# State-space inputs computed with channels on partitions and reloaded in place, and one block of the memory split a slot sooner, in a four-layer decoder trunk

## The chip, the cores and the metric

The kernel runs on one core of one Trainium2 chip, in one launch. The metric is the device time of the whole program in microseconds (us). Unmarked times are us from the start of the profiled span, or durations.

## What is computed

256 tokens of width 2048 pass through two layers, each with a mixer, a cross-attention into 256 memory tokens and an MLP of width 8192; all is float32. The first mixer is attention and retention. The second, in which most of the change lies, takes 1024 channels `u` of its input projection into a state-space bank (64 groups of 16 channels, 64 complex states each) and the rest into a gated short convolution. Cut to what matters:

```
def odd_mixer(xn, w_in, ...):
    proj = xn @ w_in
    u, h, gb, gc = jnp.split(proj, cuts, axis=-1)
    ssm = s5_mixer(u, a_re, a_im, b_re, b_im, c_re, c_im, d_skip, log_step, w_glu)
    conv = short_conv_mixer(h, gb, gc, conv_w).astype(xn.dtype)
    return jnp.concatenate([ssm, conv], axis=-1) @ w_out

# in s5_mixer: one group's channels c, states p, tokens l
    bu = jnp.einsum('blgc,gpc->blgp', uf.astype(jnp.complex64), b_bar)
    # states: x[l] = a_bar * x[l-1] + bu[l]
    y = jnp.einsum('blgp,gcp->blgc', states, c_mat).real + d_skip.astype(F32) * uf
```

At the start, `memn = rmsnorm(mem, norm_mem)` is projected by `xa_wkv` for the keys and values of both layers' cross-attention.

## The kernel before

**Weights.** Every projection streams its weights in units of 4 MB. A unit is eight halves of 512 KB, in a ring of four halves (`RING`). For each half ACT makes `whi`, the weight rounded to float32r (`split`, L1288), DVE makes `wlo = raw - whi` (L1854), and PE multiplies `x_hi*whi + x_hi*wlo + x_lo*whi`. SP loads raw slabs of two halves (L404) when the halves they replace are split. PE waits for `lo_ready` before each half; ACT may split half n once PE has finished half n-4. All the engines' programs are written out by hand, one slot for each half, and each engine works its own list in order. So what an engine waits for in a slot stands ahead of its part in the next half's weights.

**Kinds of unit.** "full" (L619 to L645) has tokens on the output's partitions: 12 matmuls of 128x512 for a half, into one bank pair of `acc`. "wide" (L1059 to L1088) and "heads" (`hidden_unit`, L1090 to L1112) have the output's channels on partitions, the weights stationary, and `x_hi`, `x_lo` side by side as the 512 moving columns: 8 matmuls of 128x512 and 8 of 128x256 for a half. Their two halves of 256 columns are then added by DVE (`hidden_sum`, L2214 and L2223). A wide unit fills two banks of `at` and one pair of `acc`, a heads unit four banks of `acc`. Both are used in the MLP: each MLP opens with a wide unit and goes on with a heads unit.

**The odd mixer.** Its projection is eight units (`O_UNITS`), the first two for `u`; t counts their halves from 0, eight to a unit. A row's 1/rms (`rstd` row 4) is ready only late in the first unit, so it scales the outputs. Before the change all eight are full. The two `u` units come out with tokens on partitions, ACT scales them into `onat` (L1306), POOL writes them to DRAM (`uc_d`, L2727), SP reads them back 128 rows at a time (`Ucb`, L543), PE turns each by two transposes (`s5_u`, L1176, after halves t = 25 to 32), ACT copies them to `UT` (L1704), and PE multiplies `UT` by the tables (`s5_x`, tile `at`, L726, after halves 27 to 34). SP's loads of the tables `et_d` (L548) wait for PE's earlier `s5_x`.

**The start.** The first unit (`first_unit`) projects the memory. PE turns the memory's four blocks of 512 columns (L702) between halves: block 0 before half 0, block 1 after half 0, block 2 after half 2, block 3 after half 4. ACT and DVE split each turned block (`hi_parts` L1320, `lo_parts` L1874) in a slot of their own; the second, block 1, in slot 2. After half 1 PE also turns the rows of gains (L742, L743) into the same two banks of `tp`, and needs them free.

The few lines that order the split of the memory's blocks on ACT:

```
    if u == 0 and i == 0:
        hi_parts(yt, 0, MEM, (1,))
    if u == 0 and i in (2, 4, 6):
        hi_parts(yt, 2 * i, MEM)
```

Of the kernel before, what the change touches and what calls it, by code (L numbers as in the profile page):

```python
# [105 lines left out]
def trunk(nc, x, mem, norm_mix, norm_xattn, norm_mlp, norm_mem, norm_final, ab_w_in, ab_b_forget,  # L106
# [4 lines left out]
    with ctx:  # L111
# [104 lines left out]
        Ucb = [view(4160 + 256 * b, 256, "p (r w) -> p r w", r=2) for b in range(3)]  # L216
# [34 lines left out]
        uc_d = nc.dram_tensor("uc_d", [G, L, GC], F32, kind="Internal").ap()  # L251
# [50 lines left out]
        uc_in, et_in = ([sem(f"{n}{b}") for b in range(3)] for n in ("uc_in", "et_in"))  # L302
# [35 lines left out]
        at_before_x = at_before_tab + 16  # L338
# [4 lines left out]
        tp_before_u = 3 + 2 * (4 + 4 + 2 + 8 + 2) + 8 + 16 + 2 * 12 + 8  # L343
# [52 lines left out]
        def _(sp):  # L396
# [53 lines left out]
            def factor_loads(s):  # L450
# [82 lines left out]
            def s5_loads(s):  # L533

                ks = [k for k in (s - X8_T - 6, s - X8_T - 5) if 0 <= k < 8]
                for k in ks:
                    if k == 0:
                        sp.wait_ge(u_out, 64)
                        for b in range(2):
                            sp.wait_ge(et_out[b], 16 * 8)  # L540
                    if k >= 3:
                        sp.wait_ge(tp_full, tp_before_u + k - 2)
                    sp.dma_start(Ucb[k % 3], uc_d.rearrange("(s q) (j i) c -> (q j) s (i c)", s=2, i=T8)[  # L543
                        P * k:P * (k + 1)]).then_inc(uc_in[k % 3], 16)
                for k in ks:
# [20 lines left out]
            for o, (name, g) in enumerate(O_UNITS):  # L566
                load("full", cd_w_in[0], [O_COL[name] + g * NB], hook=lambda i, o=o: s5_loads(8 * o + 2 * i))
# [2226 lines left out]
```

## Time and profile before

| what | value |
|---|---|
| median of 3 runs | 2427.01 us (2426.27 to 2429.1) |
| the profiled execution's own time | 2426.3 us |
| its span | 2424.5 us |
| mean granted TensorE clock | 0.998 |
| PE busy | 2407.5 us, 99% of the span |
| DVE, ACT, POOL busy | 1478.8, 1189.2, 362.2 us (61%, 49%, 15%) |
| DMA | 488.96 MB, mean 202 GB/s |

The profiled execution took 2426.3 us, 1.8 us more than its span; the sum of the prediction is made against it. PE is busy nearly all the time, so the time is the sum of what PE does and the little that it waits. Rows of the timeline merge neighbouring instructions of one kind: start, duration from the first's start to the last's end, engine, line, output and inputs, count, and in brackets the idle time before with what ended it. Matmuls overlap, so the pace is the distance between starts.

### The profile page before, as it was taken

How to read it: one execution, taken by the hardware profiler on the slowest of the kernel's cores; microseconds unless marked ns; L12 is line 12 of the kernel's file. 1: busy time of each engine (PE TensorE's matmuls, PEld its weight loads, DVE VectorE, ACT ScalarE, POOL GpSimd, SP SyncE). 2: the span in 40 equal slices, each digit the busy share in tenths (PEclk: the TensorE clock that was granted, in tenths of full speed). 3: DMA queues.
4: the chain of work that ended last, by engine and by line, in shares of the span. 5: the costliest groups of instructions: out<-in, count | busy, mean ns of one | idle time of the engine just before them, and what ended most of it. 6: DMA issues, size and time to landing. Idle time of an engine off the chain costs nothing.

```text
span 2424.5 us, 32116 instructions
## 1 busy us (share of the span) xinstructions
PE 2407.5 (99%) x12596; PEld 2023.5 (83%) x12596; DVE 1478.8 (61%) x1856; ACT 1189.2 (49%) x1583; POOL 362.2 (15%) x480
## 2 busy tenths in 40 slices
PE   9999999999999999999999999999999999999998
PEld 7878888888888888888888887788888888888887
DVE  5546554556665556888866457566755655555555
ACT  6544455546544444444445444556644444444444
POOL 0033120010564002555510100000000000000000
PEclk9999999999999999999999999999999999999999
DMA  8655555574566567787785768955565565565563
GB/s 303 213 175 180 183 205 173 161 204 141 191 191 191 190 200 222 240 260 242 249 270 178 204 230 240 264 191 155 193 191 191 190 190 190 190 190 190 190 191 122
DMA packets 335593, 488.96 MB, mean 202 GB/s; under 512 B 18517, under 2 KB 175093, under 8 KB 335349
## 3 DMA queue, kind: packets, MB, share of 16 engines
q1 hardware_dynamic: 316804, 461.47, 59.5%
q0 software_dynamic: 3920, 12.84, 2.0%
q10 hardware_dynamic: 14752, 13.05, 1.6%
q8 instruction: 79, 1.29, 0.2%
q14 instruction: 38, 0.30, 0.0%
HBM read 471.39 MB, written 20.13 MB: 203 GB/s over the span
## 4 chain that ended last, share of the span: by engine, by line
PE 93%; DVE 3%; ACT 2%; DMA 1%; issue 1%; SPq 0%; ACTq 0%; DVEq 0%
PE acc L635 19%; PE acc L637 19%; PE acc L636 19%; PE acc L1104 18%; PE acc L1107 9%; PE tp L702 2%; PE at L726 2%; DVE wlo L1854 1%; ACT whi L1288 1%; PE acc L1076 1%; PE at L1076 1%; ACT arena L1452 1%; PE tp L726 0%; DMA raw<-in_xa_wkv 0%; DMA arena<-uc_d 0%
## 5 line engine op out<-in xcount | busy, mean ns | idle before, releaser
L1854 DVE TENSOR_TENSOR wlo<-raw,whi 128x1024 fp32r<-128x1024 f32 x824 | 1043.5, 1270 | 834.7 <-ACT whi L1288 831.1
L1288 ACT ACTIVATE whi<-raw 128x1024 fp32r<-128x1024 f32 x824 | 871.2, 1061 | 978.0 <-PE acc L637 597.2
L635 PE MATMUL acc<-whi,yt_hi 128*128 128x512 f32 x1408 | 553.3, 393 | 0.7 <-DVE h L1891 0.4
L637 PE MATMUL acc<-whi,yt_lo 128*128 128x512 f32 x1408 | 548.4, 389 | 0.0
L636 PE MATMUL acc<-wlo,yt_hi 128*128 128x512 f32 x1408 | 548.2, 389 | 0.0
L1104 PE MATMUL acc<-x,whi 128*128 128x512 f32 x1920 | 481.7, 393 | 0.0
L1104 PEld LDWEIGHTS acc<-x,whi 128*128 128x128 f32 x1920 | 345.9, 189 | 64.3 <-issue 1.6
L635 PEld LDWEIGHTS acc<-whi,yt_hi 128*128 128x128 f32 x1408 | 264.4, 188 | 57.3 <-issue 2.0
L637 PEld LDWEIGHTS acc<-whi,yt_lo 128*128 128x128 f32 x1408 | 264.3, 188 | 55.7
L636 PEld LDWEIGHTS acc<-wlo,yt_hi 128*128 128x128 f32 x1408 | 264.5, 188 | 53.1
L635 PE MATMUL acc<-whi,x 128*128 128x512 f32 x736 | 292.8, 398 | 0.9 <-DVE wlo L1854 0.9
L637 PE MATMUL acc<-whi,x 128*128 128x512 f32 x736 | 287.1, 390 | 0.0
L636 PE MATMUL acc<-wlo,x 128*128 128x512 f32 x736 | 286.6, 389 | 0.0
L1107 PEld LDWEIGHTS acc<-x,wlo 128*128 128x128 f32 x1920 | 261.9, 190 | 18.7
L1107 PE MATMUL acc<-x,wlo 128*128 128x256 f32 x1920 | 267.7, 282 | 0.0
L2480 POOL TENSOR_TENSOR arena<-arena 128x32 f32<-128x32 f32 (+5 forms) x275 | 191.0, 695 | 319.5 <-DMA arena<-fp_d 181.2
L635 PEld LDWEIGHTS acc<-whi,x 128*128 128x128 f32 x736 | 138.2, 188 | 32.4 <-DVE wlo L1854 4.0
L637 PEld LDWEIGHTS acc<-whi,x 128*128 128x128 f32 x736 | 138.1, 188 | 29.6
L636 PEld LDWEIGHTS acc<-wlo,x 128*128 128x128 f32 x736 | 138.4, 188 | 27.2
L2750 POOL TENSOR_TENSOR arena<-h,arena 128x1024 f32<-128x1024 f32 x2 | 5.7, 2846 | 662.1 <-DVE h L1891 662.1
L1891 DVE SCALAR_TENSOR_TENSOR h<-acc,rstd,h 128x512 f32<-128x512 f32 x124 | 87.0, 743 | 0.0
L2223 DVE TENSOR_REDUCE arena<-acc 128x256 f32<-128x512 f32 x124 | 84.7, 683 | 0.0
(240 smaller groups left out, 1517.8 us busy)
## 6 DMA issues: line engine op xcount, KB each, us to landing
raw<-in_mlp_w SPq DMA_DIRECT2D x256, 1024.0 KB, 5.6
raw<-in_ab_w_in SPq DMA_DIRECT2D x56, 1024.0 KB, 4.9
raw<-in_cd_w_in SPq DMA_DIRECT2D x32, 1024.0 KB, 5.4
raw<-in_ab_w_out SPq DMA_DIRECT2D x16, 1024.0 KB, 5.0
raw<-in_cd_w_out SPq DMA_DIRECT2D x16, 1024.0 KB, 6.4
raw<-in_xa_wkv SPq DMA_DIRECT2D x15, 1024.0 KB, 6.4
raw<-in_xa_wq SPq DMA_DIRECT2D x16, 512.0 KB, 4.5
ca_d<-arena ACTq DMA_DIRECT2D x16, 288.0 KB, 6.4
```

The lines of the kernel that those rows point to most:

```text
L635: pe.matmul(a, xh, whi[:, w, kk], start=opens and kk == 0, stop=False)
L636: pe.matmul(a, xh, wlo[:, w, kk], start=False, stop=False)
L637: last = pe.matmul(a, xl, whi[:, w, kk], start=False, stop=closes and kk == 1)
L702: last = pe.transpose(bank[:, kk * L + t * P:kk * L + (t + 1) * P], src[:, t, (2 * b + kk) * P:(2 * b + kk + 1) * P], ident[:, :])
L726: return pe.matmul(o, lhsT, rhs, start=start, stop=stop)
L1104: pe.matmul(o.rearrange("p (a n) -> p a n", a=2), w_hi[:, kk, :], x2[:, :, k0 + kk, :], start=i < 4 and kk == 0, stop=False)
L1107: last = pe.matmul(o[:, 0:L], w_lo[:, kk, :], x2[:, 0, k0 + kk, :], start=False, stop=i >= 4 and kk == 7)
L1288: act.activation(split_weights(whi, kind, i), half_weights(raw, kind, i), ACT.Copy)\
L1854: dve.tensor_tensor(split_weights(wlo, kind, i), half_weights(raw, kind, i), split_weights(whi, kind, i).bitcast(F32), ALU.subtract).then_ ...
L1891: last = dve.scalar_tensor_tensor(out=hb, in0=acc[:, 2 * par_ + t, :], scalar=rstd[:, row, t:t + 1], in1=hb, op0=ALU.mult, op1=ALU.add)
L2223: ins = dve.tensor_reduce(hid[:, hh, :], bank.rearrange("p (a n) -> p n a", a=2), AX.X, ALU.add)
L2480: link(pool.tensor_tensor(o, a, b, op))
```

## The change

The two `u` units become a wide and a heads unit (`O_KIND`), so that `u` comes out with channels on partitions. DVE's new `u_block` adds the two halves of each bank and multiplies by `srow`, a row of 1/rms over the tokens that every partition holds, with the tokens reordered. POOL makes that row from `rstd`: a write to DRAM (`r_d`), a broadcast read (`row4`) and two copies. POOL then writes each half of `u` to DRAM (`u_d`) and reads it straight into `UT`, 16 channels by 8 token phases on the partitions. SP's `uc_d` loads, PE's 16 transposes and ACT's copies and scalings of `u` fall away. The order of partitions in the tables (`fac`, `t_d`) follows; no instruction is added there. ACT's and DVE's split of the memory's block 1 moves from slot 2 to slot 1.

```
@@ -213,7 +213,10 @@
         S = view(2112, 2048, "p (r j q) -> p r j q", r=2, q=Q)
-        Ucb = [view(4160 + 256 * b, 256, "p (r w) -> p r w", r=2) for b in range(3)]
+        row4 = view(4160, L)
+        srow = view(4416, L, "p (i j) -> p i j", i=T8)
+        usum = [view(4672 + L * v, L) for v in range(2)]
+        uT = view(9408, 1024, "p (b i j) -> p b i j", b=4, i=T8)
         Yc = view(4160, 1024, "p (b i n) -> p b i n", p=2 * J, b=YB, i=T8)
@@ -248,7 +251,8 @@
         k_d = nc.dram_tensor("k_d", [GC, G, 240], F32, kind="Internal").ap()
-        uc_d = nc.dram_tensor("uc_d", [G, L, GC], F32, kind="Internal").ap()
+        u_d = nc.dram_tensor("u_d", [2, Q * GC, L], F32, kind="Internal").ap()
+        r_d = nc.dram_tensor("r_d", [1, L], F32, kind="Internal").ap()
         kv_d = nc.dram_tensor("kv_d", [2, P, 1024], F32, kind="Internal").ap()
@@ -320,6 +325,7 @@
         O_UNITS = [("u", 0), ("u", 1), ("h", 0), ("gc", 0), ("gb", 0), ("h", 1), ("gc", 1), ("gb", 1)]
+        O_KIND = ["wide", "heads"] + 6 * ["full"]
         O_COL = {"u": 0, "h": 1024, "gb": 2048, "gc": 3072}
@@ -467,9 +473,9 @@
                     for f, v in enumerate((fb_d, fp_d)):
-                        rows = v[:, 2 * k:2 * k + 2].rearrange("m q r w -> m (q r w)").unsqueeze(1 if f else 0)
+                        rows = v[:, 2 * k:2 * k + 2].rearrange("m q r w -> m (q r w)").unsqueeze(0 if f else 1)
                         sp.dma_start(fac[:, k % 2, f].rearrange("p q r w -> p (q r w)"),
-                                     rows.to_broadcast([T8, GC, 512])).then_inc(f_in[k % 2], 16)
+                                     rows.to_broadcast([GC, T8, 512])).then_inc(f_in[k % 2], 16)
@@ -535,14 +541,8 @@
                     if k == 0:
-                        sp.wait_ge(u_out, 64)
                         for b in range(2):
                             sp.wait_ge(et_out[b], 16 * 8)
-                    if k >= 3:
-                        sp.wait_ge(tp_full, tp_before_u + k - 2)
-                    sp.dma_start(Ucb[k % 3], uc_d.rearrange("(s q) (j i) c -> (q j) s (i c)", s=2, i=T8)[
-                        P * k:P * (k + 1)]).then_inc(uc_in[k % 3], 16)
-                for k in ks:
                     if k >= 3:
@@ -564,7 +564,7 @@
             for o, (name, g) in enumerate(O_UNITS):
-                load("full", cd_w_in[0], [O_COL[name] + g * NB], hook=lambda i, o=o: s5_loads(8 * o + 2 * i))
+                load(O_KIND[o], cd_w_in[0], [O_COL[name] + g * NB], hook=lambda i, o=o: s5_loads(8 * o + 2 * i))
             for o in range(2):
@@ -1164,23 +1164,12 @@
-            u_tok = {}
-
-            def s5_u(k):
-
-                Uc = Ucb[k % 3]
-                assert p.n["tp"] == tp_before_u + k, p.n["tp"]
-                pe.wait_ge(uc_in[k % 3], 16 * (k // 3 + 1))
-                bank = open_tp()
-                for r in range(2):
-                    last = pe.transpose(bank[:, r * P:(r + 1) * P], Uc[:, r, :], ident[:, :])
-                u_tok[k] = close_tp(last)
-
             def s5_x(k):
-                wait_tp_read(pe, u_tok.pop(k))
                 if k == 0:
                     pe.wait_ge(ut_zero, 1)
+                    for s in range(2):
+                        pe.wait_ge(u_in[s], 16)
                 ETc = ETb[k % 3]
@@ -1212,8 +1201,6 @@
                     s5_x(t - X8_T - 2)
-                if 0 <= t - X8_T < 8:
-                    s5_u(t - X8_T)
                 if 0 <= t - Y_T < 16:
@@ -1232,7 +1219,9 @@
-            for o in range(8):
+            wide_unit(x_tok, lambda i: odd_after(0, i))
+            hidden_unit(x_tok, lambda i: odd_after(1, i))
+            for o in range(2, 8):
                 unit("full", xt, x_tok, lambda i, o=o: odd_after(o, i))
@@ -1405,8 +1394,8 @@
                         hi_parts(yt, 0, MEM, (1,))
-                    if u == 0 and i in (2, 4, 6):
-                        hi_parts(yt, 2 * i, MEM)
+                    if u == 0 and i in (1, 4, 6):
+                        hi_parts(yt, 2 * max(i, 2), MEM)
                     if u == 0 and i == 3:
@@ -1697,13 +1686,6 @@
             def s5_slots(t):
-                k = t - 3 - X8_T
-                if 0 <= k < 8:
-                    act.wait_ge(tp_full, p.at("tp", 1))
-                    b = p.n["tp"] % 2
-                    act.activation(UT[:, :, 4 * k:4 * k + 4, :], tp[:, b, 0:2 * 4 * J].rearrange(
-                        "p (r q j) -> p r q j", q=4, r=2), ACT.Copy).then_inc(tp_free[b], 1)
-                    p.bump("tp")
                 k = t - 5 - X8_T
@@ -1731,15 +1713,11 @@
                 if prev and i == (2 if prev[0] == "gb" else 3):
-                    if prev[0] == "u":
-                        if prev[1]:
-                            act.wait_ge(u_out, 32)
-                        scaled(onat, 4)
-                    elif prev[0] == "h":
+                    if prev[0] == "h":
                         scaled(hn, 4)
...
                         if prev[1] == 0:
-                            act.wait_ge(u_out, 64)
+                            act.wait_ge(u_out, 32)
                         scaled(onat, 4)
@@ -1756,8 +1734,9 @@
                 act.wait_ge(ca_out[b], 16 * 8)
+            p.bump("at", 2)
             for o in range(8):
-                unit("full", lambda i, o=o: odd_slots(o, i))
+                unit(O_KIND[o], lambda i, o=o: odd_slots(o, i))
@@ -1977,8 +1956,8 @@
                         lo_parts(yt, 0, MEM, banks=(1,))
-                    if u == 0 and i in (2, 4, 6):
-                        lo_parts(yt, 2 * i, MEM)
+                    if u == 0 and i in (1, 4, 6):
+                        lo_parts(yt, 2 * max(i, 2), MEM)
                     if u == 0 and i == 3:
@@ -2351,6 +2330,33 @@
+            def u_block(g, hh):
+
+                both = usum[hh % 2]
+                back = 1 if g == 0 else 2 - hh // 2
+                par_ = parity(p, back)
+                if g == 0 and hh < 2:
+                    n = at_before_u + hh
+                    dve.wait_ge(at_full, n + 1)
+                    bank = at[:, n % 2, :]
+                else:
+                    dve.wait_ge(*((wide_done, 2) if g == 0 and hh == 2 else
+                                  (half_used, p.at("half", hh - 3 if g else 0))))
+                    bank = acc[:, 2 * par_ + hh % 2, :]
+                total = dve.tensor_reduce(both, bank.rearrange("p (a n) -> p n a", a=2), AX.X, ALU.add)
+                if g == 0 and hh < 2:
+                    total.then_inc(at_free[n % 2], 1)
+                    dve.wait_ge(at_free[n % 2], n // 2 + 1)
+                elif hh % 2:
+                    total.then_inc(acc_free[par_], 1)
+                    wait_freed(dve, p, back)
+                else:
+                    link(total)
+                if hh == 0:
+                    dve.wait_ge(*((u_out, 16) if g else (r_ready, 1)))
+                dve.tensor_tensor(uT[:, hh], both.rearrange("p (j i) -> p i j", i=T8), srow, ALU.mult)\
+                   .then_inc(u_ready, 1)
+
             def odd_slots(o, i):
@@ -2359,6 +2365,11 @@
                         rms(4, root_count(4))
+                if o == 1 and i == 1:
+                    for hh in range(4):
+                        u_block(0, hh)
+                if o == 2 and i < 4:
+                    u_block(1, i)
                 prev = O_UNITS[o - 1] if 1 <= o <= 8 else None
@@ -2716,17 +2725,25 @@
             for i in range(T8):
-                pool.dma_start(t_d[i * GC:(i + 1) * GC], k_d[:, :, 112 - GC * i:240 - GC * i]).then_inc(t_out, 16)
-
-
+                pool.dma_start(t_d.rearrange("(c i) g w -> i c g w", i=T8)[i], k_d[:, :, 112 - GC * i:240 - GC * i]).then_inc(t_out, 16)
+
+
+            pool.wait_ge(rstd_ready, 5)
+            pool.dma_start(r_d[0].rearrange("(p t) -> p t", t=TOK), rstd[:, 4, :]).then_inc(r_out, 16)
+            pool.wait_ge(r_out, 16)
+            pool.dma_start(row4, r_d.to_broadcast([P, L])).then_inc(r_in, 16)
+            pool.wait_ge(r_in, 16)
+            spread = row4.rearrange("p (j i t) -> p t i j", i=T8, t=TOK)
+            link(pool.tensor_copy(srow[:, :, 0:J // 2], spread[:, 0]))
+            pool.tensor_copy(srow[:, :, J // 2:J], spread[:, 1]).then_inc(r_ready, 1)
             for g in range(2):
-                wait_block(OB + g)
+                pool.wait_ge(u_ready, 4 * (g + 1))
                 if g == 0:
                     pool.memset(UT0[:, :, :, 0:1], 0.0).then_inc(ut_zero, 1)
-                for t in range(TOK):
-                    pool.dma_start(uc_d.rearrange("g (t p) c -> t p g c", t=TOK)[
-                        t, :, g * Q:(g + 1) * Q, :], onat[:, t, :].rearrange("p (g c) -> p g c", c=GC))\
-                        .then_inc(u_out, 16)
+                pool.dma_start(u_d[g].rearrange("(b p) n -> p b n", b=4), uT.rearrange("p b i j -> p b (i j)"))\
+                    .then_inc(u_out, 16)
+                pool.wait_ge(u_out, 16 * (g + 1))
+                pool.dma_start(UT[:, g], u_d[g].rearrange("(q c) (i j) -> (c i) q j", q=Q, i=T8)).then_inc(u_in[g], 16)
             for n in range(2):
```

What the edits do to the lists of instructions is seen in three places (the names in brackets are the semaphores waited for).

ACT, in the first unit, from the second part of block 0 to the gains; `yt_hi` x4 is the memory's block 1. Before:

```order
L1320 ACTIVATE yt_hi<-tp,gain 128x256 x2
L1288 ACTIVATE whi<-raw 128x1024 x2
L1320 ACTIVATE yt_hi<-tp,gain 128x256 x4
L1342 ACTIVATE junk,ssq<-arena 128x512 x2
L1288 ACTIVATE whi<-raw 128x1024
L1413 ACTIVATE gain<-tp 128x96
```

With the change:

```order
L1309 ACTIVATE yt_hi<-tp,gain 128x256 x2
L1277 ACTIVATE whi<-raw 128x1024
L1309 ACTIVATE yt_hi<-tp,gain 128x256 x4
L1277 ACTIVATE whi<-raw 128x1024
L1331 ACTIVATE junk,ssq<-arena 128x512 x2
L1277 ACTIVATE whi<-raw 128x1024
L1402 ACTIVATE gain<-tp 128x96
```

The block's four parts stood behind the weights of half 2, and now stand ahead of them.

DVE, odd mixer, from the end of 1/rms at t = 7 on; `usum` and `uT` are parts of the arena. Before, nothing stands between the weights of halves 8 and 9 and those of half 10:

```order
L1898 TENSOR_REDUCE nrm<-ssq 128x2 [waits ssq_ready]
L1899 TENSOR_SCALAR nrm<-nrm 128x2 [waits dve_step]
L1854 TENSOR_TENSOR wlo<-raw,whi 128x1024 [waits hi_ready]
L1906 RECIPROCAL nrm<-nrm 128x2 [waits sd_ready]
L1907 TENSOR_TENSOR nrm<-nrm 128x2 [waits dve_step]
L1908 SCALAR_TENSOR_TENSOR nrm<-nrm 128x2 [waits dve_step]
L1909 SCALAR_TENSOR_TENSOR rstd<-nrm 128x2 [waits dve_step]
L1854 TENSOR_TENSOR wlo<-raw,whi 128x1024 [waits hi_ready] x28
L2369 SCALAR_TENSOR_TENSOR arena<-acc,rstd,arena 128x512 [waits acc_free1,half_used]
```

With the change:

```order
L1888 SCALAR_TENSOR_TENSOR rstd<-nrm 128x2 [waits dve_step]
L1833 TENSOR_TENSOR wlo<-raw,whi 128x1024 [waits hi_ready] x2
L2346 TENSOR_REDUCE arena<-at 128x256 [waits at_full]
L2357 TENSOR_TENSOR arena<-arena 128x256 [waits r_ready,at_free1]
L2346 TENSOR_REDUCE arena<-at 128x256 [waits at_full]
L2357 TENSOR_TENSOR arena<-arena 128x256 [waits at_free0]
L2346 TENSOR_REDUCE arena<-acc 128x256 [waits wide_done]
L2357 TENSOR_TENSOR arena<-arena 128x256 [waits dve_step]
L2346 TENSOR_REDUCE arena<-acc 128x256 [waits half_used]
L2357 TENSOR_TENSOR arena<-arena 128x256 [waits acc_free1]
L1833 TENSOR_TENSOR wlo<-raw,whi 128x1024 [waits hi_ready] x7
```

Eight instructions, the second of which waits for POOL's row, stand ahead of the weights of half 10.

POOL, after the tables (`t_d`). Before:

```order
L2719 DMA t_d<-k_d 1024x128 x7
L2725 MEMSET arena 128x64 [waits acc_free1]
L2727 DMA uc_d<-arena 128x32x16 x2
L2727 DMA uc_d<-arena 128x32x16 [waits acc_free0]
L2727 DMA uc_d<-arena 128x32x16
L2731 MEMSET yt_hi 128x2048
```

With the change:

```order
L2732 DMA r_d<-rstd 128x2 [waits rstd_ready]
L2734 DMA arena<-r_d 128x256 [waits r_out]
L2737 COPY arena<-arena 128x8x16 [waits r_in]
L2738 COPY arena<-arena 128x8x16 [waits pool_step]
L2742 MEMSET arena 128x64 [waits u_ready]
L2743 DMA u_d<-arena 128x4x256
L2746 DMA arena<-u_d 128x32x32 [waits u_out]
L2743 DMA u_d<-arena 128x4x256 [waits u_ready]
L2746 DMA arena<-u_d 128x32x32 [waits u_out]
L2748 MEMSET yt_hi 128x2048
```

Each step of POOL's chain now waits for the one before it, two of them for a transfer.

## Rows read from the trace of the kernel before

**Rows 1.** PE's waits over the whole span: us in total, times, longest

```profile
PE tp L742 <- DVE yt_lo L1874: 1.5, 1, 1.5
...
PE tp L1176 <- DMA arena<-uc_d: 1.1, 1, 1.1
```

**Rows 2.** Timeline of PE, first unit, halves 0 to 3 (start, us, what)

```profile
11.08 1.04 PE L702 MATMUL tp<-ident,arena 128*128 128x128 f32 x8
...
13.80 1.07 PE L612 MATMUL acc<-wlo,yt_hi 128*128 128x512 f32 x4
16.34 0.28 PE L742 MATMUL tp<-ident,arena 96*128 96x96 f32 x1 [1.47 <-DVE yt_lo L1874]
17.03 0.24 PE L743 MATMUL tp<-ident,arena 24*128 24x24 f32 x1 [0.42 <-DVE yt_lo L1874]
17.20 1.84 PE L605 MATMUL acc<-whi,yt_hi 128*128 128x512 f32 x4
...
21.64 1.04 PE L702 MATMUL tp<-ident,arena 128*128 128x128 f32 x8
```

**Rows 3.** Stretches of the start: busy time of each engine, then PEclk, DMA share, GB/s

```profile
14.00:17.50 3.50, 1.61 (x7) 0.95 (x6) 2.79 (x5) 3.50 (x10) 0.00 (x0) 1.00 1.05 387
17.50:21.00 3.50, 3.50 (x10) 2.69 (x9) 2.39 (x2) 1.43 (x4) 0.00 (x0) 0.51 1.06 381
```

**Rows 4.** Timeline of ACT, first unit: weights of halves 1 and 2, block 1

```profile
9.08 1.06 ACT L1288 ACTIVATE whi<-raw 128x1024 fp32r<-128x1024 f32 x1
13.09 1.06 ACT L1288 ACTIVATE whi<-raw 128x1024 fp32r<-128x1024 f32 x1 [2.94 <-DMA raw<-in_xa_wkv]
14.05 1.55 ACT L1320 ACTIVATE yt_hi<-tp,gain 128x256 fp32r<-128x256 f32 x4
```

**Rows 5.** The third weight slab (halves 4 and 5): its issue, and its landing

```profile
L404 SPq DMA_DIRECT2D raw<-in_xa_wkv x1: 477/477/477, 7.3 to 7.3; - x1
...
DMA to landing us min/median/max: 9.9/9.9/9.9
```

**Rows 6.** Timeline of PE, odd mixer: t = 3 begins, transposes after t = 25, 26

```profile
1332.91 0.47 PE L635 MATMUL acc<-whi,x 128*128 128x512 f32 x1
...
1395.61 0.38 PE L1176 MATMUL tp<-ident,arena 128*128 128x128 f32 x2
...
1398.59 0.38 PE L1176 MATMUL tp<-ident,arena 128*128 128x128 f32 x2
```

**Rows 7.** Timeline of PE, first MLP: wide unit's last five halves, then heads unit

```profile
610.64 0.70 PE L1076 MATMUL at<-x,whi 128*128 128x512 f32 x2
...
624.65 2.00 PE L1104 MATMUL acc<-x,whi 128*128 128x512 f32 x8
...
634.12 2.00 PE L1104 MATMUL acc<-x,whi 128*128 128x512 f32 x8
...
648.08 0.40 PE L635 MATMUL acc<-whi,yt_hi 128*128 128x512 f32 x1
```

**Rows 8.** Timeline of DVE, first MLP, around the same change of units

```profile
619.04 0.16 DVE L1909 SCALAR_TENSOR_TENSOR rstd<-nrm 128x2 f32<-128x2 f32 x1
...
622.76 1.39 DVE L2214 TENSOR_REDUCE arena<-at 128x256 f32<-128x512 f32 x2 [0.96 <-PE at L1079]
...
625.46 1.22 DVE L1854 TENSOR_TENSOR wlo<-raw,whi 128x1024 fp32r<-128x1024 f32 x1
```

**Rows 9.** Timeline of POOL, first layer: a small write to DRAM and what waited

```profile
225.34 0.58 POOL L2544 DMA_DIRECT2D c_d<-c  x1 [0.29 <-POOL arena L2530]
228.15 1.12 POOL L2504 DMA_DIRECT2D arena<-in_decay  x2 [2.24 <-DMA c_d<-c]
```

**Rows 10.** DMA issues of POOL: count, KB each, us from issue to landing

```profile
uc_d<-arena POOLq DMA_DIRECT2D x4, 256.0 KB, 9.3
...
arena<-in_s_b_re POOLq DMA_DIRECT2D x2, 128.0 KB, 4.9
...
arena<-y_d POOLq DMA_DIRECT2D x2, 128.0 KB, 3.7
```

**Rows 11.** Groups of POOL by line and shape: busy us, mean ns

```profile
L2673 POOL COPY a<-arena 128x32 f32<-128x32 f32 x2 | 1.3, 650 | 0.1
```

**Rows 12.** Timeline of DVE, odd mixer: one product of 128x256

```profile
1445.84 0.42 DVE L2323 TENSOR_TENSOR arena<-arena,a 128x256 f32<-128x256 f32 x1
```

More of the change, by code:

```diff
@@ L301, in trunk @@
         u_out = sem("u_out")
-        uc_in, et_in = ([sem(f"{n}{b}") for b in range(3)] for n in ("uc_in", "et_in"))
+        r_out, r_in, r_ready, u_ready = (sem(n) for n in ("r_out", "r_in", "r_ready", "u_ready"))
+        u_in, et_in = [sem(f"u_in{s}") for s in range(2)], [sem(f"et_in{b}") for b in range(3)]
         ca_in = [sem(f"ca_in{b}") for b in range(4)]
@@ L337, in trunk @@
         at_before_tab = at_before_factors + 3
-        at_before_x = at_before_tab + 16
+        at_before_u = at_before_tab + 16
+        at_before_x = at_before_u + 2
         at_before_y = at_before_x + 8
         gains_put = [4, 3]
-        tp_before_u = 3 + 2 * (4 + 4 + 2 + 8 + 2) + 8 + 16 + 2 * 12 + 8
         OB = 4 + 14 + 4 + 2 + 4 + 8 * CHUNKS - 1
@@ L2217, in hidden_sum @@
                     if wide and hh == 2:
-                        dve.wait_ge(wide_done, layer + 1)
+                        dve.wait_ge(wide_done, 1 + 2 * layer)
                     else:
@@ L2297, in _ @@
             mlp(0, 3, MIX + 16, False, s5_params, re_tables)
-            p.bump("at", 3 + 16)
+            p.bump("at", 3 + 16 + 2)
             def convolve(g):
@@ L2382, in odd_slots @@
                     lo_parts(yt, 8 + 4 * prev[1], src=cv)
-                if 0 <= t - 3 - X8_T < 8:
-                    p.bump("tp")
                 if 0 <= t - SCAN_T < SCAN_STEPS:
@@ L2388, in _ @@
             for o in range(8):
-                unit("full", lambda i, o=o: odd_slots(o, i))
+                unit(O_KIND[o], lambda i, o=o: odd_slots(o, i))
             def conv_adds(i, n):
@@ L2740, in _ @@
                                    y_d[s].rearrange("(t p) n -> p t n", p=P)[:, :, c0:c1]).then_inc(y_in[s], 16)
-            wait_block(OB + 8 + 4 + 2 + 4 + 2 + 4)
+            wait_block(OB + 9 + 4 + 2 + 4 + 2 + 4)
             pool.dma_start(gfin, norm_final.rearrange("(a n) -> a n", a=1).to_broadcast([P, D]))\
@@ L2747, in _ @@
             for b in range(2):
-                wait_block(OB + 8 + 4 + 2 + 4 + 2 + 4 + 8 * CHUNKS - 1 - 4 + b)
+                wait_block(OB + 9 + 4 + 2 + 4 + 2 + 4 + 8 * CHUNKS - 1 - 4 + b)
                 c = slice(b * NB, (b + 1) * NB)
```

## The prediction

> **What bounds the kernel now.** I read the waits of PE first. PE is busy in 99% of the span, and its own list of waits is short: the longest two that the change touches are 1.5 us before the gains' transposes at the start and 1.1 us before one of the state-space transposes [rows 1]. So the time is PE's list of work plus a few small holes. A change pays only if it takes work off PE's list, fills a hole, or keeps PE's clock up; time saved on ACT, SP or POOL is worth nothing by itself. A hole opens where PE waits for `lo_ready`, and DVE and ACT work their lists in order, so I read next what stands ahead of the weights in their lists.
>
> **The start: block 1 split in slot 1.** PE ends half 1 at 14.87 (13.80 + 1.07). Then it stands: the gains' transposes start at 16.34 and 17.03, each after DVE has cleared a bank, and half 2 starts at 17.20 [rows 2]. DVE is late because ACT is. ACT ended half 1's weights at 10.14, stood 2.94 us for the slab of half 2 (13.09), and only then took block 1, from 14.05 to 15.60 [rows 4]. But block 1 was turned by 12.12 (11.08 + 1.04) [rows 2]. With the block ahead of the slab's wait, ACT takes the first bank at about 11.7 and is done at about 13.3 (1.55 us of work, spread over both banks), and DVE follows by about 14.2. Half 2's weights move from 13.09 to about 13.3, done at 14.4. The transposes of the gains then follow half 1 directly and half 2 starts at about 15.1 instead of 17.20: **2.1 us** gained.
>
> There is a second gain. The granted clock is 1.00 from 14.0 to 17.5 and 0.51 from 17.5 to 21.0 [rows 3], so PE ran at the lower of its two levels, 1.2 GHz, right after the stretch in which it was busy for 1.61 of 3.50 us. Half 2 took 4.44 us, from 17.20 to 21.64 [rows 2]. At the full clock a half is 2.73 us: 23 halves from 1332.91 to 1395.61 [rows 6]. With the hole gone PE works without a break from 8 us on, and I expect no fall: **1.7 us** more.
>
> Does what comes later keep up? The third slab lands at 17.2 (7.3 + 9.9) [rows 5]. PE wants half 4 at 15.1 + 2 x 2.73 + 0.8 for eight transposes = 21.4. ACT needs one split of 1.06 and block 2's 1.55 in between [rows 4], so 4 us are enough. DMA is saturated here (share 1.05 [rows 3]), so the slabs of the second unit will not land 3.8 us sooner; they have the ring of four halves, 11 us, as cover. If that cover were gone, the 3.8 us would be handed back one for one.
>
> **The two units for `u`.** In the first MLP the wide unit's last five halves take 14.01 us (610.64 to 624.65), 2.80 each, and the heads unit's last five 13.96 (634.12 to 648.08), 2.79 each [rows 7]. Full halves take 2.73 [rows 6]. Eight of each kind: 8 x 0.07 + 8 x 0.06 = **1.1 us lost**.
>
> **The transposes that go.** From the pair after t = 25 to the pair after t = 26 it is 2.98 us, against 2.73 for a half alone [rows 6]: 0.25 us for a pair. Eight pairs: **2.0 us gained**. With them goes the wait for `uc_d`, **1.1 us** [rows 1]. What is late next at that place is the table `et_d`. Its loads wait for PE's `s5_x` of three steps before, as now, and no longer stand behind two loads of `uc_d` on SP, so I put nothing in the wait's place. ACT's copies and scalings that fall away, and SP's shorter list, are worth nothing: they stand beside PE. The other order of partitions in `fac` and `t_d` moves the same bytes and is priced at nothing; its cover is the rest of the MLP, some 80 us.
>
> **The wait that comes.** This decides the sign of the remainder. DVE must do eight instructions between halves 9 and 10, and the second waits for POOL's row of 1/rms. Behind it stand half 10's weights, which PE needs. The same change of units in the MLP gives the calendar. 1/rms is ready at 619.20, the heads unit starts at 624.65 [rows 7, 8], and its third half could start 2 x 2.79 later, at 630.23 (in that place nine extra transposes put it off): 11.0 us from the one to the other. In the MLP four reductions from 622.76 fit well, and the weights of half 10 start at 625.46 [rows 8]. In the odd mixer the chain from 1/rms is:
>
> - POOL's write of the row. A small write took 2.81 us from its issue to the next instruction, which waited for it [rows 9].
> - POOL's broadcast read of 128 KB. POOL's loads of that size land after 3.7 and 4.9 us [rows 10]; I take 4.0.
> - Two copies of 128x128. The only near row is a copy of 128x32 at 0.65, the first of its kind [rows 11]; I take 0.5 each, 1.0.
> - One product of 0.42 [rows 12], then three times a reduction (1.39 / 2 = 0.70 [rows 8]) and a product: 0.42 + 3 x 1.1 = 3.7.
> - Half 10's weights, 1.2 [rows 8].
>
> Sum 12.7 against 11.0: PE stands **1.7 us** before half 10. Ends: none at all with a write of 2.0, a read of 3.7 and copies of 0.2 each (2.0 + 3.7 + 0.4 + 3.7 + 1.2 = 11.0); with the write and the read both as slow as POOL's slowest kind of transfer, 9.3 us each [rows 10], it would be 9.3 + 9.3 + 1.0 + 3.7 + 1.2 - 11.0 = 13.5. I take the value from the small transfers, since both are small.
>
> The Trainium skill's page "DMA: Bandwidth & Descriptors", section "Anatomy of one DMA — SWDGE (gpsimd) path", prices a transfer issued by GpSimd at a fixed 2.0 us plus its bytes at 436 GB/s. That would be an estimated 4.3 us for the two steps, so there would be no stall and the sum would be 1.7 us lower. The trace does not agree for the small write: 2.81 us for 8 KB [rows 9].
>
> **The read back.** `UT` must be there when PE has ended t = 27, two halves after 1395.61 [rows 6], which is 54 us after the heads unit's start (20 halves). The last product of `u` comes some 27 us after it: eight halves, one weights' subtraction, reduction and product, and the stall. The write has 512 pieces of 1 KB, the read 4096 of 128 bytes. `uc_d` had 4096 pieces of 64 bytes and took 9.3 us [rows 10]; twice that is 18.6, so it is in place 8 us early. Priced at nothing.
>
> **The sum.** -2.1 - 1.7 + 1.1 - 2.0 - 1.1 + 1.7 = -4.1 us, from the profiled execution's 2426.3 to 2422.2. The median of the runs shown is 0.7 above that execution, so I say **2422.9 us**, 0.17% less. A measurement of this kernel can tell about 0.2% from no change, 4.9 us: the forecast is just inside.
>
> **The rivals.**
>
> *The row comes in time.* DVE's wait ends before PE wants half 10. For it: the bytes are few, and the chain is only 1.7 us too long. Against: each of the rows above would have to be at its low end at once. Sum -5.8, 2421.2 us, faster by 0.24%.
>
> *The start gives only the hole.* The clock falls somewhere else in the first 20 us, or in typical runs of before it does not fall as it did in the profiled one. For it: the 1.7 us rest on one stretch of one execution [rows 3]. Sum -2.4, 2424.6 us.
>
> *The start gives nothing.* ACT waits for the turned block in slot 1 and that pushes half 2's weights back, or the change of slot frees no bank sooner, so it doesn't do what it says. Against: the block was turned at 12.12, before the slab landed. Sum -0.3, 2426.7 us.
>
> *A long stall.* The chain takes 3 to 7 us more than I say, PE stands 5 to 9 us before half 10, and its clock falls after that hole as it did at the start, 1.7 us more: -5.8 + 5 + 1.7 = +0.9 at the near end, 2427.9 us.
>
> *Slower.* The same place and mechanism, from the point where the row is ready over 15 us after 1/rms instead of 7.8: the stall passes 9 us, and with the clock's 1.7 it outweighs the 5.8 gained by over 4.9. With both transfers at 9.3 us it is -5.8 + 13.5 + 1.7 = +9.4, 2436.4 us. For it: each step waits for the one before, behind weight slabs on busy DMA engines. Against: rows 9.
>
> **How the numbers follow.** Forecast 0.38, row in time 0.25, only the hole 0.20, nothing at the start 0.04, long stall 0.08, slower 0.05. Faster by over 0.2% are most of "row in time" and the lower third of the forecast's own spread (a stall of 0.7 us or less): 0.36. Slower by over 0.2% is the last case and a rest: 0.06. Same: 0.58. The range reaches from 1.2 us under "row in time", for the spread between runs, to 2426.8, which takes in the start that gives nothing and the stalls of up to some 4 us with a fallen clock: 2420.0 to 2426.8.
>
> **What would show it.** Right: PE's waits at the gains' transposes are gone, the clock is 1.00 from 14 to 21, half 2 takes 2.7 us; DVE's first product of `u_block` starts some 7.8 us after 1/rms and PE waits 1 to 3 us before half 10; no transposes and no wait at t = 25 to 32; the two `u` units take 22.4 us each. Wrong: no PE wait before half 10; a low clock in the first 40 us or after half 10; PE waiting before the first `s5_x` (the read back) or for `et_d`; slabs of the second unit arriving late.

## The result and the profile after

| | before | with the change |
|---|---|---|
| median | 2427.43 us (2424.74 to 2430.37, 21 runs) | 2430.99 us (2429.61 to 2432.24, 21 runs) |
| profiled execution; its span | 2426.3; 2424.5 us | 2430.99; 2429.2 us |
| mean granted clock | 0.998 | 0.997 |

The ratio is 1.0015, 95% interval 1.0009 to 1.0021, against the executions of before that ran beside it; every ratio below is made so. The change costs 3.6 us. That is less than the 0.2% that the forecast counts as no change, but the measured time lies 4.2 us above the top of its range, and the sign is not the one forecast.

PE's own list of waits after the change, in us in total, times, longest:

```profile
PE acc L1104 <- DVE wlo L1833: 8.0, 1, 8.0
PE tp L726 <- DVE yt_lo L2018: 1.4, 4, 0.4
```

Both waits of [rows 1] are gone. One new wait of 8.0 us stands at the head of the list. It is the wait before half 10 of the odd mixer, where the forecast had 1.7.

The start on PE, which answers to [rows 2], and the first unit's end:

```profile
14.70 0.25 PE L742 MATMUL tp<-ident,arena 96*128 96x96 f32 x1
14.88 0.24 PE L743 MATMUL tp<-ident,arena 24*128 24x24 f32 x1
15.04 1.19 PE L605 MATMUL acc<-whi,yt_hi 128*128 128x512 f32 x4
...
17.91 0.82 PE L702 MATMUL tp<-ident,arena 128*128 128x128 f32 x6
...
34.23 0.39 PE L635 MATMUL acc<-whi,yt_hi 128*128 128x512 f32 x1
```

On ACT, which answers to [rows 4], block 1 now stands ahead of the weights of half 2:

```profile
11.71 1.57 ACT L1309 ACTIVATE yt_hi<-tp,gain 128x256 fp32r<-128x256 f32 x4 [1.61 <-PE tp L702]
13.27 1.06 ACT L1277 ACTIVATE whi<-raw 128x1024 fp32r<-128x1024 f32 x1
```

And the stretches, with the columns of [rows 3]: the two of the start, and three at the new wait.

```profile
14.00:17.50 3.50, 3.50 (x17) 2.69 (x16) 2.44 (x3) 2.82 (x9) 0.00 (x0) 1.00 1.05 390
17.50:21.00 3.50, 3.50 (x21) 3.00 (x20) 2.77 (x6) 3.41 (x8) 0.00 (x0) 1.00 1.06 381
1344.00:1352.00 8.00, 4.96 (x30) 4.22 (x28) 0.66 (x2) 2.60 (x3) 1.32 (x3) 0.97 0.50 70
1352.00:1357.00 5.00, 0.04 (x1) 0.07 (x1) 4.89 (x8) 0.00 (x0) 0.87 (x2) 0.50 0.00 0
1357.00:1362.00 5.00, 5.00 (x16) 4.23 (x17) 3.22 (x3) 0.00 (x0) 1.70 (x1) 0.53 0.86 270
```

The start came as forecast: half 2 begins at 15.04 instead of 17.20 and takes 2.87 us instead of 4.44, at a clock of 1.00. From 1352 the reader sees the other side: PE stands, its clock is at the lower level (0.50, which is 1.2 GHz), and it is still there for most of the next 5 us of full work (0.53).

The chain that PE waits for, on POOL:

```profile
1338.07 0.61 POOL L2732 DMA_DIRECT2D r_d<-rstd  x1 [103.47 <-DVE rstd L1888]
1345.34 0.55 POOL L2734 DMA_DIRECT2D arena<-r_d  x1 [6.67 <-DMA r_d<-rstd]
1350.39 0.39 POOL L2737 COPY arena<-arena 128x128 f32<-128x128 f32 x1 [4.50 <-DMA arena<-r_d]
1350.84 0.39 POOL L2738 COPY arena<-arena 128x128 f32<-128x128 f32 x1
```

on DVE:

```profile
1337.62 0.16 DVE L1888 SCALAR_TENSOR_TENSOR rstd<-nrm 128x2 f32<-128x2 f32 x1
...
1341.33 0.69 DVE L2346 TENSOR_REDUCE arena<-at 128x256 f32<-128x512 f32 x1 [1.16 <-PE at L1079]
1351.34 0.61 DVE L2357 TENSOR_TENSOR arena<-arena 128x256 f32<-128x256 f32 x1 [9.31 <-POOL arena L2738]
1351.87 0.68 DVE L2346 TENSOR_REDUCE arena<-at 128x256 f32<-128x512 f32 x1
```

and on PE:

```profile
1347.85 1.11 PE L1107 MATMUL acc<-x,wlo 128*128 128x256 f32 x8
1356.96 3.75 PE L1104 MATMUL acc<-x,whi 128*128 128x512 f32 x8 [7.99 <-DVE wlo L1833]
...
1362.01 1.99 PE L1104 MATMUL acc<-x,whi 128*128 128x512 f32 x8
```

Half 10 takes 5.05 us (1356.96 to 1362.01) where a heads half takes 2.79. So the hole costs its 8.0 us and, at the lower clock behind it, 5.05 - 2.79 = 2.3 us more.

To see where the time went I set the start of the same matmul in two traces against each other, counted from the first matmul up to the odd mixer and from the last behind it (the change has 48 matmuls more). The table gives how much later it is than in the trace of before (us), at places named by the time in before. `e1`, `e2` and `e4` are experiments told of below: the memory's slot alone, the rest of the change alone, and the change with its products moved.

```
place in before        e1      e2      change    e4
  91.7               -3.84   +0.06     -3.77   -3.26
 975.8               -3.84   +0.04     -3.78   -3.24
1274.4               -3.12   -0.36     -3.87   -3.22
1420.6               -4.29   +7.19     +4.94   -4.81
2371.7               -4.32   +7.03     +4.76   -4.93
```

The change leads by 3.8 us until the odd mixer, loses 8.8 between 1274 and 1421, and nothing moves after that.

### The profile page after: what moved, and what is told of

It reads as the page before. It is cut to its first block, busy times and chain, and to the rows that moved or that the text cites. A ratio compares the mean times of both kernels' runs of the same rounds, so it can differ in the third digit from the quotient of the medians.

```text
span 2429.2 us, 32218 instructions
## 1 busy us (share of the span) xinstructions
PE 2407.2 (99%) x12644; PEld 2025.7 (83%) x12644; DVE 1488.2 (61%) x1872; ACT 1184.8 (49%) x1571; POOL 361.1 (15%) x484
## 4 chain that ended last, share of the span: by engine, by line
PE 93%; DVE 4%; ACT 2%; DMA 1%; issue 1%; ACTq 0%; SPq 0%; POOL 0%; DVEq 0%
PE acc L635 19%; PE acc L637 19%; PE acc L636 19%; PE acc L1104 18%; PE acc L1107 9%; PE at L726 2%; PE tp L702 2%; DVE wlo L1833 2%; ACT whi L1277 1%; PE acc L1076 1%; PE at L1076 1%; ACT arena L1441 1%; PE tp L726 0%; PE acc L985 0%; PE acc L983 0%
## 5 line engine op out<-in xcount | busy, mean ns | idle before, releaser
L1104 PE MATMUL acc<-x,whi 128*128 128x512 f32 x1984 | 499.6, 394 | 8.2 <-DVE wlo L1833 8.0
L1104 PEld LDWEIGHTS acc<-x,whi 128*128 128x128 f32 x1984 | 358.4, 189 | 75.1 <-issue 9.6
L1107 PEld LDWEIGHTS acc<-x,wlo 128*128 128x128 f32 x1984 | 271.3, 191 | 19.5
L1107 PE MATMUL acc<-x,wlo 128*128 128x256 f32 x1984 | 277.1, 283 | 0.0
L635 PE MATMUL acc<-whi,x 128*128 128x512 f32 x672 | 267.5, 398 | 0.9 <-DVE wlo L1833 0.9
L637 PE MATMUL acc<-whi,x 128*128 128x512 f32 x672 | 262.1, 390 | 0.0
L636 PE MATMUL acc<-wlo,x 128*128 128x512 f32 x672 | 261.9, 390 | 0.0
L635 PEld LDWEIGHTS acc<-whi,x 128*128 128x128 f32 x672 | 126.2, 188 | 30.3 <-DVE wlo L1833 3.8
L637 PEld LDWEIGHTS acc<-whi,x 128*128 128x128 f32 x672 | 126.1, 188 | 26.9
L636 PEld LDWEIGHTS acc<-wlo,x 128*128 128x128 f32 x672 | 126.3, 188 | 24.8
```

Of the source, the lines that this page charges most:

```text
L635: pe.matmul(a, xh, whi[:, w, kk], start=opens and kk == 0, stop=False)
L636: pe.matmul(a, xh, wlo[:, w, kk], start=False, stop=False)
L637: last = pe.matmul(a, xl, whi[:, w, kk], start=False, stop=closes and kk == 1)
L1104: pe.matmul(o.rearrange("p (a n) -> p a n", a=2), w_hi[:, kk, :], x2[:, :, k0 + kk, :], start=i < 4 and kk == 0, stop=False)
L1107: last = pe.matmul(o[:, 0:L], w_lo[:, kk, :], x2[:, 0, k0 + kk, :], start=False, stop=i >= 4 and kk == 7)
```

## The experiments

**1. The memory's slot alone.** The kernel before, with block 1 split in slot 1 on ACT and DVE:

```
-                    if u == 0 and i in (2, 4, 6):
-                        hi_parts(yt, 2 * i, MEM)
+                    if u == 0 and i in (1, 4, 6):
+                        hi_parts(yt, 2 * max(i, 2), MEM)
```

> The kernel before with one part of the change: the memory's block 1 is split in slot 1. Theory A (the change's loss is all in one stall before half 10, with the low clock behind it; the start gives what was forecast): 3.8 us less than before, some 2422.5 us in a profiled execution and about 2423.6 in the median, no wait before the gains' transposes, half 2 in 2.7 us. Theory B (the start's second gain, the clock, was an accident of one execution): in the median only the hole of 2.1 us is gained, about 2425.3.

Measured 2422.7 us (2421.34 to 2426.06, 11 runs) against 2426.7 (28 runs), ratio 0.9985, interval 0.9976 to 0.9994. The median is 4.0 us lower, where theory B had 1.4; so the start's gain is not an accident of one execution. The trace is 3.8 us ahead after the start and 4.3 at the end. The clock goes with the slot: at the start it stays at 1.00 here, and in number 2, which has the old slot, it falls again.

```profile
17.50:21.00 3.50, 3.50 (x21) 2.94 (x21) 2.70 (x6) 3.50 (x8) 0.00 (x0) 1.00 1.05 381
```

```profile
17.50:21.00 3.50, 3.50 (x11) 2.74 (x11) 2.39 (x2) 1.51 (x4) 0.00 (x0) 0.66 1.06 379
```

The first row is from number 1, the second from number 2. The trace of number 1 also shows no wait for `uc_d`, though `uc_d` is still used: the lead grows by 1.2 us between 1274 and 1421. So that wait depends on when the transfers fall, and that it is gone after the full change proves nothing about the change.

**2. The rest without the memory's slot.** The changed kernel with the four lines above put back.

> The change without its edit of the memory's split. Theory A: the stall of 8.0 us and 2.3 us of low clock stay, so +1.1 - 2.0 - 1.1 + 10.3 = +8.3 us against before, about 2435.5 us. Theory B (the loss comes in part from how the two parts meet, as weights arriving late after a shorter start): clearly less than +8, down to +5.

Measured 2433.8 us (2431.01 to 2435.74, 10 runs), ratio 1.0027, interval 1.0018 to 1.0037. Its PE waits:

```profile
PE acc L1104 <- DVE wlo L1833: 7.1, 1, 7.1
PE tp L742 <- DVE yt_lo L1853: 1.8, 1, 1.8
```

The loss of 7.1 us lies between the two theories, and its own trace accounts for it: the stall is 7.1 us instead of 8.0, and half 10 takes 4.64 us (1359.60 to 1364.24), 1.9 more than 2.79, so +1.1 - 2.0 - 1.1 + 7.1 + 1.9 = +7.0. The state-space part alone loses 7.1 us, the slot alone wins 4.0: 3.1 together, and the whole change lost 3.6. The parts add up.

**3. The row made one row of 1/rms earlier.** POOL sends row 3 of `rstd`, ready since the MLP, instead of row 4, so nothing waits for it in the mixer (the state-space inputs are scaled by the wrong row).

```
-            pool.wait_ge(rstd_ready, 5)
-            pool.dma_start(r_d[0].rearrange("(p t) -> p t", t=TOK), rstd[:, 4, :]).then_inc(r_out, 16)
+            pool.wait_ge(rstd_ready, 4)
+            pool.dma_start(r_d[0].rearrange("(p t) -> p t", t=TOK), rstd[:, 3, :]).then_inc(r_out, 16)
```

> The change with POOL's row made from the 1/rms of the norm before (row 3 of rstd instead of row 4), so that it is ready long before DVE asks; the state-space inputs are scaled by the wrong row. The same instructions otherwise. Theory A: no wait before half 10 and no low clock; the change without its stall, 10.3 us less than the change: about 2420.7 us, 5.8 under the profiled before, ratio 0.9975. Theory B (the two units, the reloads or DVE's eight instructions cost more than I priced, whatever the row does): some us of wait remain, 2423 or more.

Measured 2422.16 us (2421.52 to 2425.01, 11 runs), ratio 0.9981, interval 0.9972 to 0.9990. There is no wait before half 10. Without the late row the change is faster than before, so the row's lateness is the whole loss. The median is 1.5 us above theory A's 2420.7. The profiled execution was the slowest of the eleven, and shows another hole, in the MLP at 1259.76, and a longer wait for the memory's blocks at the start (0.2 us in the change):

```profile
PE acc L1104 <- DVE arena L2202: 1.8, 1, 1.8
PE tp L702 <- DMA arena<-in_mem: 1.6, 1, 1.6
```

Before the hole ACT had waited 6.2 us for a weight slab. Shortly before stand POOL's eight `t_d` transfers, 4 MB, and one slab of that stretch landed 21.6 us after its issue; the slowest took 18.2 with the change as it is and 18.6 in the kernel before. Whether the row's own transfers, which fall into that stretch only here, made the difference is not shown, nor whether the other executions have such a hole. The half after the 1.8 us hole took 4.32 us instead of 2.79 (1259.76 to 1264.08).

```profile
1259.76 2.81 PE L1104 MATMUL acc<-x,whi 128*128 128x512 f32 x8 [1.77 <-DVE arena L2202]
1262.37 1.91 PE L1107 MATMUL acc<-x,wlo 128*128 128x256 f32 x8
1264.08 2.14 PE L1104 MATMUL acc<-x,whi 128*128 128x512 f32 x8
```

**4. The products later.** The four sums stay in slot 1, in four buffers instead of two. The wait for the row and the four products go to slot 5. All is computed.

```
-        usum = [view(4672 + L * v, L) for v in range(2)]
+        usum = [view(4672 + L * v, L) for v in range(4)]
...
                 if o == 1 and i == 1:
                     for hh in range(4):
-                        u_block(0, hh)
+                        u_sum(0, hh)
+                if o == 1 and i == 5:
+                    for hh in range(4):
+                        u_product(0, hh)
```

> The change with DVE's part in two: the four sums stay in slot 1 of the second unit (they free the banks), into four buffers instead of two, and the four products with the row, and the wait for it, move four slots on, to slot 5. All is computed. Theory A: the row is ready 13.5 us after 1/rms, before DVE reaches slot 5, so PE waits for nothing: the same time as with the row made early, about 2420.7 us, and faster than before by 0.25%. Theory B (DVE's products delay weights wherever they stand, or the row comes later still): 1 to 5 us more.

Measured **2420.81 us** (2419.82 to 2422.15, 7 runs), ratio 0.9972, interval 0.9961 to 0.9983: faster than both kernels, 10.2 us under the change as it stands, and 0.1 from what theory A said. The chain is no shorter here, only nobody waits for it:

```profile
1338.72 0.61 POOL L2741 DMA_DIRECT2D r_d<-rstd  x1 [103.57 <-DVE rstd L1888]
1346.16 0.55 POOL L2743 DMA_DIRECT2D arena<-r_d  x1 [6.83 <-DMA r_d<-rstd]
```

```profile
1343.47 1.42 DVE L2355 TENSOR_REDUCE arena<-acc 128x256 f32<-128x512 f32 x2
1344.92 2.36 DVE L1833 TENSOR_TENSOR wlo<-raw,whi 128x1024 fp32r<-128x1024 f32 x2
...
1352.73 2.38 DVE L2337 TENSOR_TENSOR arena<-arena 128x256 f32<-128x256 f32 x4 [0.76 <-POOL arena L2747]
```

The weights of half 10 are made at 1344.92, eight us before the row is there.

**5 to 8. Why the row is late.** These four look at the chain itself. The row's write is 1 KB in 128 pieces of 8 bytes, two tokens from each partition, and it is issued while weight slabs are in flight. Number 5 writes 1 KB to the same place in two pieces of 512 bytes; two rows of the identity stand in for 1/rms, so the inputs are scaled by wrong numbers, and the source is two partitions instead of 128:

```
-            pool.dma_start(r_d[0].rearrange("(p t) -> p t", t=TOK), rstd[:, 4, :]).then_inc(r_out, 16)
+            pool.dma_start(r_d[0].rearrange("(p n) -> p n", n=P), ident[0:2, :]).then_inc(r_out, 16)
```

> The change with another source for POOL's small write: the same 1 KB to DRAM, but as two rows of 512 bytes of the identity matrix instead of 128 pieces of 8 bytes of rstd (the inputs are scaled by rows of the identity). It still waits for 1/rms. Theory P (128 pieces of 8 bytes are what made the write take 7.0 us): it lands after about 2.5 to 3 us, as the 8 KB in eight rows did in the first layer, the row is ready 4 us sooner and PE's wait before half 10 falls from 8.0 to about 4. Theory Q (the write stands among the weight slabs that are in flight): still 6 to 7 us and a wait of 7 to 8.

Numbers 6 and 7 keep the slabs away, first from the write, then from the read too (`r_in` in place of `r_out`):

```
                     if kind == "heads":
+                        if w is cd_w_in0 and i == 3:
+                            sp.wait_ge(r_out, 16)
```

> The change, and SP holds the last weight slab of the second unit (and so the first of the third) until the small write has landed; nothing else. Both slabs have over 14 us to spare before ACT wants them. Theory Q: the write lands after 2.5 to 3 us on idle DMA engines, the wait before half 10 falls to 4 or 5 us (the broadcast read now meets the slabs), some 4 us less than the change in all. Theory P: the write still takes 7 us, the wait is unchanged.

> As the last, but SP holds the slabs until the broadcast read has landed too. Theory Q: write 2.5 to 3 us and read 3 to 5 us with nothing else in flight; row ready some 9 us after 1/rms instead of 13.5, wait before half 10 about 3.5 us, and with it less of the low clock or none: about 5 us less than the change, 2425 to 2426 us. Theory P: write 7 us, a wait of 7 to 8 us.

Number 8 has the edits of 5 and 7 together.

> The change with both edits to the relay at once: the row is written as two rows of 512 bytes instead of 128 pieces of 8 bytes (rows of the identity stand in for 1/rms, so the state-space inputs are scaled by other numbers), and SP starts no weight slab until the row has been read back. It is the fourth corner of a square: 8-byte pieces beside weight slabs landed after 7.0 us, 8-byte pieces with idle queues after 3.5, 512-byte pieces beside slabs after 4.6. Theory A (small pieces are slow only because each waits in turn among the slabs' pieces): with idle queues the size of the pieces is worth nothing, the write lands after 3.3 to 3.6 us, the read after 4.2 as with 8-byte pieces and idle queues, and PE stands 3.6 to 4.0 us before half 10. Theory B (a small piece has a price of its own, whatever else flows): the write lands after 2.3 us or less, as far under 3.5 as 4.6 is under 7.0, PE stands 1.3 to 2.8 us. In either case the forecast's 1.7 us of stall is the best that this chain could do. Time: A 2426.5 to 2427.5 us, B 2424.5 to 2425.5. If the clock falls after this hole too, a stall costs some 2.5 us beyond its own length.

| | write lands after | read lands after | PE waits | half 10 takes | median, ratio (interval) |
|---|---|---|---|---|---|
| the change | 7.0 | 5.0 | 8.0 | 5.05 | 2430.99, 1.0015 (1.0009 to 1.0021) |
| 5, two pieces | 4.6 | 3.4 | 4.1 | 5.26 | 2427.6, 1.0005 (0.9996 to 1.0015) |
| 6, hold for write | 3.6 | 8.5 | 8.1 | 4.74 | 2431.0, 1.0019 (1.0009 to 1.0029) |
| 7, hold for row | 3.5 | 4.2 | 3.8 | 5.13 | 2426.86, 1.0000 (0.9990 to 1.0009) |
| 8, both | 1.6 | 3.2 | 1.0 | 2.87 | 2421.67, 0.9981 (0.9971 to 0.9990) |

The landings are the two ends of the row of the tile `r_d` (us, min/median/max of its two transfers). In the change and in numbers 5 and 8:

```profile
DMA to landing us min/median/max: 5.0/6.0/7.0
```

```profile
DMA to landing us min/median/max: 3.4/4.0/4.6
```

```profile
DMA to landing us min/median/max: 1.6/2.4/3.2
```

In numbers 6 and 7:

```profile
DMA to landing us min/median/max: 3.6/6.0/8.5
```

```profile
DMA to landing us min/median/max: 3.5/3.9/4.2
```

POOL's next instruction tells which is which: in the change it waits 6.67 us behind the write and 4.50 behind the read. The write is the 7.0, 4.6, 1.6, 3.6 and 3.5.

Neither theory of numbers 5 to 7 holds alone. The pieces account for a part (4.6, where P had 2.5 to 3 and Q 6 to 7) and the slabs for a part. Of number 8 theory B holds for the write. With 8-byte pieces, keeping the slabs away takes the write from 7.0 to 3.5 us. With 512-byte pieces it goes from 4.6 to 1.6. So the slabs cost 3.0 to 3.5 us and the small pieces 1.9 to 2.4, each whatever the other does. Three traces with 8-byte pieces beside slabs (the change, numbers 2 and 4) have 7.0, 7.1 and 7.2, two with the slabs held 3.5 and 3.6; the two values with 512-byte pieces rest on one execution each, and the number of source partitions changed along with the pieces. The Trainium skill's page "DMA: Bandwidth & Descriptors", section "Specifications", puts the least piece for full rate at 512 bytes and says that below it the DMA engine reads and modifies what it writes; these runs agree in direction (1.9 to 2.4 us dearer with 8-byte pieces) and don't show the mechanism. Number 6 missed its forecast of a wait of 4 or 5 us, and shows the trade that experiments on one transfer fall into: the write gained 3.4 us, the slabs that had been held then ran beside the read, and it lost 3.5. Number 7 has the wait about as forecast (3.8 against 3.5) and the write 0.5 us longer than Q's 2.5 to 3; the low clock stayed (half 10 takes 5.13), and the median is 0.9 us above Q's 2425 to 2426.

Number 8's PE, at the place of the change's 5.05 us:

```profile
PE acc L1108 <- DVE wlo L1837: 1.0, 1, 1.0
```

```profile
1349.80 2.08 PE L1108 MATMUL acc<-x,whi 128*128 128x512 f32 x8 [0.97 <-DVE wlo L1837]
1352.67 2.00 PE L1108 MATMUL acc<-x,whi 128*128 128x512 f32 x8
```

```profile
1348.00:1358.00 10.00, 9.03 (x53) 7.83 (x53) 7.51 (x7) 3.18 (x3) 2.59 (x3) 1.00 1.00 342
```

This wait of 1.0 us left the clock at 1.00. It is shorter than the 1.3 us at which theory B ended, so the forecast's 1.7 was not the best that this chain could do, and with no low clock behind it the median is 2.8 us under B's range. Behind number 5's hole of 4.1 us the half took 5.26:

```profile
1352.42 3.75 PE L1104 MATMUL acc<-x,whi 128*128 128x512 f32 x8 [4.09 <-DVE wlo L1833]
1355.97 1.91 PE L1107 MATMUL acc<-x,wlo 128*128 128x256 f32 x8
1357.68 2.05 PE L1104 MATMUL acc<-x,whi 128*128 128x512 f32 x8
```

So the lower clock costs 2.5 us behind a hole of 4.1 and 2.3 behind one of 8.0 (numbers 7, 2 and 6: 2.3 behind 3.8, 1.9 behind 7.1, 2.0 behind 8.1): from 3.8 us on a longer hole costs no more. Between number 8 and number 5 the hole grew by 3.1 us and the median by 5.9.

## Why the prediction was wrong

**The start (-2.1, -1.7): right.** Half 2 starts 2.16 us sooner and takes 1.57 less. The 3.8 us are kept to the odd mixer; no slab of the second unit came late.

**The two units (+1.1), the transposes (-2.0), the wait for `uc_d` (-1.1): right in sum.** A heads half takes 2.79 behind the stall too (1364.79 to 1367.58). Experiment 4, which has no stall, goes from -3.22 to -4.81 between 1274 and 1421, -1.6 for the three terms, where the forecast has -2.0. They were not measured one by one. The third is in part luck: in experiment 1 the wait is gone with `uc_d` still in place.

**The read back: right.** PE has no wait before the first `s5_x`, nor for `et_d`.

**The wait that comes (+1.7): this step failed, by the price of POOL's small write.** The wait measured +8.0. Link by link, from 1/rms at 1337.78 to half 10 at 1356.96:

| link | forecast | measured |
|---|---|---|
| to POOL's issue | 0 | 0.29 |
| write, issue to next instruction | 2.81 | 7.27 |
| read, the same | 4.0 | 5.05 |
| copies, and to DVE | 1.0 | 0.95 |
| products and sums | 3.7 | 4.26 |
| half 10's weights | 1.2 | 1.36 |
| sum | 12.7 | 19.2 |
| room until PE wants half 10 | 11.0 | 11.2 |

Of the 6.5 us that the chain was too short, 4.5 are the write, 1.1 the read and 1.0 the rest. The write's price came from one row, `c_d` [rows 9]. That write is 8 pieces of 1 KB; this one is 128 of 8 bytes. And the forecast left out what is in flight at 1338, where the DMA share is 1.04 over the whole write (first row, from the change). The row of `c_d` is not free of traffic either, but it met only the end of it (the other rows, from before; its write is issued at 225.34 and lands after 2.5 us):

```profile
1338.00:1345.00 7.00, 7.00 (x40) 6.04 (x39) 2.83 (x3) 3.03 (x3) 0.61 (x1) 1.00 1.04 271
```

```profile
225.00:226.00 1.00, 1.00 (x6) 0.84 (x5) 1.00 (x1) 0.26 (x1) 0.62 (x2) 1.00 1.04 403
226.00:227.00 1.00, 1.00 (x6) 0.81 (x6) 1.00 (x2) 0.02 (x1) 0.00 (x0) 1.00 1.03 397
227.00:228.00 1.00, 1.00 (x6) 0.84 (x5) 0.26 (x1) 1.00 (x1) 0.00 (x0) 1.00 0.08 27
```

There one slab had 2.4 us left when the write was issued; here one slab was issued 1 us before the write and another 2 us after it. How much of the 2.5 us that slab's end cost is not shown. The forecast named the risk in its last rival ("behind weight slabs on busy DMA engines") and gave it 0.05 against that one row. The products take 0.61, not the 0.42 of [rows 12]: small, but missed four times. They read their input in another order than that product does; whether this is why is not shown.

**The clock behind the stall: left out of the sum.** Of the forecast's cases only the long stalls, from some 4 us on, have a fallen clock; behind its own 1.7 us it has none, and gives no reason. The start [rows 2, 3] had shown it fall behind two waits of 1.5 and 0.4 us, and that was the evidence for 1.7 us of gain there; the same reading was not applied to the loss. With a stall of 8.0 the term is +2.3; in experiment 3 a hole of 1.8 us, about the forecast's own size, cost 1.5 behind it.

With both terms as measured the sum is -2.1 - 1.7 + 1.1 - 2.0 - 1.1 + 8.0 + 2.3 = +4.5 us, and the profiled execution is 4.7 longer. The rival "A long stall" had the mechanism: by its own formula, -5.8 + 8.0 + 1.7 = +3.9, it gives 2430.9 for the median, which is what was measured (2430.99). It had a chance of 0.08, because the price of the write was trusted. The place and the order of the chain were read rightly; what was mis-sized is that link.

What stays open: the read landed after 4.2 us in number 7 and 3.2 in number 8, both with the slabs held, and after 5.0 in the change and 3.4 in number 5, both beside slabs. It is the same read of the same 1 KB; only the write before it differs. One execution of each doesn't say whether that is chance.

## What to carry to other kernels

Price a small transfer on the path by its pieces and by what is in flight when it is issued, not by its bytes: 1 KB took 1.6 to 7.2 us here in the mixer. Where an engine that works in order must wait for such a relay, put the work that doesn't need it, and the next tile's weights, ahead of the wait; moving the wait and four products by four slots was worth some 10 us, from 2430.99 to 2420.81. And price a hole in PE twice, once by its length and once by the clock behind it: here that second price was there from 1.8 us on, and not at 1.0.

## What the hardware showed beyond that

- A write of 1 KB: 7.0 to 7.2 us as 128 pieces of 8 bytes beside slabs of 1 MB, 3.5 and 3.6 with none in flight, 4.6 as two pieces of 512 bytes beside slabs, 1.6 with neither. In experiment 3 the 8-byte write, issued in the MLP before the mixer, behind 4 MB of `t_d`, took 17.3.
- What the lower clock cost in the half behind a hole: less than 0.1 us behind 1.0, 1.5 (4.32 - 2.79) behind 1.8, 2.3 and 2.5 behind 3.8 and 4.1, 1.9, 2.3 and 2.0 behind 7.1, 8.0 and 8.1.
- Slabs of 1 MB that land in 5.5 us when alone took up to 18.6, 18.2 and 21.6 beside POOL's eight transfers of `t_d` (before, the change, number 3).
